# Three landing buffers instead of four for the streamed weights of a two-block transformer kernel

## The reference

```python
for layer in range(2):                       # first_block
    x = x + 0.5 * swiglu(rmsnorm(x), ffn1_w_in, ffn1_w_out)
    x = x + (attn_lru_mixer, deltanet_mixer)[layer](rmsnorm(x))
    x = x + cross_attention(rmsnorm(x), rmsnorm(mem))
    x = x + 0.5 * swiglu(rmsnorm(x), ffn2_w_in, ffn2_w_out)
x = rmsnorm(x)
for i in range(4):                           # second_block
    u = rmsnorm(x)
    x = x + rmsnorm((retention, conformer_conv, gla)[i % 3](u))
    x = x + rmsnorm(sq_relu_mlp(rmsnorm(x), mlp_w_up[i], mlp_w_down[i]))
```

## Time and profile before

| what | value |
|---|---|
| median of the 3 runs | 2798.34 us (2797.26 to 2812.16) |
| the profiled execution's own time | 2798.34 us |
| its span, first to last instruction | 2796.6 us |
| granted TensorE clock over the span, share of full speed | 0.991 |
| PEld busy | 2605.9 us (93%) |
| DVE busy | 1810.6 us (65%) |
| ACT busy | 1410.2 us (50%) |
| weight transfers | 836 of 512 KB |
| weight queue, share of the 16 DMA engines' span | 48.9% |

### The profile page before, as it was taken

The page is one execution under the profiler, slowest core; times in us unless marked ns, Lnnn a source line. Parts: engine busy times, 40 slices in busy tenths (PEclk is TensorE's granted clock), DMA queues, the critical chain, the costliest instruction groups (busy, mean ns, idle before and its releaser), DMA issues. The chain is left out here.

```text
span 2796.6 us, 49287 instructions
## 1 busy us (share of the span) xinstructions
PE 2700.4 (97%) x21142; PEld 2605.9 (93%) x21142; DVE 1810.6 (65%) x2351; ACT 1410.2 (50%) x1928; POOL 0.2 (0%) x4
## 2 busy tenths in 40 slices
PE   7999999999998889999999999989999999999998
PEld 7999899999988889999899999879988899989998
DVE  5657766666657646666646856968555675755764
ACT  5445555454466355545445565354454544446443
POOL 0000000000000000000000000000000000000000
PEclk9999999999999999999999999989999999999999
DMA  6554546655544234655544554226642465444463
GB/s 222 177 188 144 180 134 204 196 189 189 189 129 124 76 121 136 197 186 172 182 135 145 183 194 158 68 102 190 202 148 93 149 201 197 160 149 151 160 196 120
DMA packets 129002, 450.13 MB, mean 161 GB/s; under 512 B 20112, under 2 KB 20368, under 8 KB 128528
## 3 DMA queue, kind: packets, MB, share of 16 engines
q1 hardware_dynamic: 128784, 446.96, 48.9%
HBM read 445.47 MB, written 1.44 MB: 160 GB/s over the span
## 5 line engine op out<-in xcount | busy, mean ns | idle before, releaser
L262 PE MATMUL B<-R,WH 128*128 128x256 f32 x10432 | 2077.5, 282 | 33.7 <-DVE WL L965 24.7
L262 PEld LDWEIGHTS B<-R,WH 128*128 128x128 f32 x10432 | 1673.2, 189 | 50.7 <-issue 21.9
L965 DVE TENSOR_TENSOR WL<-SL,WH 128x1024 fp32r<-128x1024 f32 x836 | 1009.4, 1223 | 743.1 <-ACT WH L2007 742.4
L262 PE MATMUL B<-R,WL 128*128 128x256 f32 x4480 | 1253.7, 280 | 0.0
L2007 ACT ACTIVATE WH<-SL 128x1024 fp32r<-128x1024 f32 x836 | 865.2, 1052 | 526.8 <-PE B L262 506.8
L262 PEld LDWEIGHTS B<-R,WL 128*128 128x128 f32 x4480 | 846.2, 189 | 0.0
L262 PE MATMUL B<-RB,WH 128*128 128x256 f32 x1984 | 553.4, 279 | 0.8 <-DVE WL L965 0.8
L262 PE MATMUL B<-RB,WL 128*128 128x256 f32 x1728 | 481.1, 278 | 0.0
L262 PEld LDWEIGHTS B<-RB,WH 128*128 128x128 f32 x1984 | 371.9, 187 | 1.3 <-DVE WL L965 1.0
L262 PEld LDWEIGHTS B<-RB,WL 128*128 128x128 f32 x1728 | 324.3, 188 | 0.0
L262 PE MATMUL B<-WH,R 128*128 128x512 f32 x480 | 159.5, 403 | 0.9 <-DVE WL L965 0.9
(11 more groups left out here) (282 smaller groups left out, 1572.4 us busy)
## 6 DMA issues: line engine op xcount, KB each, us to landing
SL<-in_w SPq DMA_DIRECT2D x836, 512.0 KB, 3.6
CP<-in_cp SPq DMA_DIRECT2D x5, 768.0 KB, 5.0
X<-in_xT SPq DMA_DIRECT2D x2, 512.0 KB, 6.6
PG<-in_mem SPq DMA_DIRECT2D x1, 1024.0 KB, 10.8
out<-X SPq DMA_DIRECT2D x1, 1024.0 KB, 3.9
PK<-in_pk SPq DMA_DIRECT2D x1, 594.5 KB, 3.7
dn_y<-PG SPq DMA_DIRECT2D x1, 256.0 KB, 2.2
PG<-dn_y SPq DMA_DIRECT2D x16, 16.0 KB, 2.1
```

What stands on the lines that cost most here:

```text
L262: return p.matmul(o, left, right, start=first, stop=final, skip_group_check=True)
L965: v.tensor_tensor(WL[t % NSPL][:, :], SL[t % NRAW][:, :], WH[t % NSPL][:, :].bitcast(F32), ALU.subtract).then_inc(s_lo, 1)
```

## The change

The number of raw buffers is lowered from four to three. `NRAW` also is the number of landing semaphores `s_w`, and it stands in the indices and counts of lines 2004, 2007, 965 and 2800 to 2802. The number of split buffers, `NSPL`, stays at four. No instruction is added, removed or moved in any engine's list. What differs is the buffer that a tile lands in, and the condition of the wait in line 2801: tile t now waits for `lo(t - 3)` where it waited for `lo(t - 4)`. The transfer of tile 3, which was issued without a wait, now waits for `lo(0)`. The program uses 4 KB less in each of the 128 partitions.

```diff
@@ -118,7 +118,7 @@
     ST, NBLOCKS = stage_table()
     NTILES = w.shape[0]
     assert NBLOCKS == 4 * NTILES
-    NRAW, NSPL = 4, 4
+    NRAW, NSPL = 3, 4
```

## The result

In the comparison the changed kernel took 2820.9 us (median, 2807.9 to 2830.5), the kernel before 2802.8 us (2788.4 to 2812.2); the ratio is 1.0063, 95% interval [1.005, 1.0077]. That is above the range of 2799 to 2818 us. Two further measurements of the changed kernel, each beside the kernel before, gave 1.0035 [1.0018, 1.0053] and 1.006 [1.0048, 1.0072]. The mean of the three is 1.0053, or 14.8 us; the forecast was 9.0 us. The reference moved as well: 2798.34 us was the median of three runs, and the later medians of the kernel before were 2800.4 to 2807.9 us.

The account below looks back on a forecast made before the run. PE, busy for 97% of the span, was taken as the bound, so delays cost only where they reach it. Five terms summing to 9.0 us, on 2798.34 us, gave 2807.3 us; 2799 to 2818 us should hold 8 times in 10.

Parts of the forecast that it names:

- the steady stretches don't see it: Where PE sets the pace, three buffers still leave about 2.8 us to spare, so no change is seen.
- no transfer gets slower: Tile t's transfer starts when that of t + 1 started before, and takes what that one took.
- forecast marks: ACT's waits for landings grow from 19.7 us to 80 to 150 us, in some 70 to 100 waits instead of 15.
- The rival of the starving lockstep: Tile pairs in mN.up lose time to late transfers, 2827 us; 21% for it or a milder form, above 2812.
- Term 1: Starts of m0.up to m3.up: the late fourth high part delays PE 1.0 us in each, 4.0 us.
- My own rule: The `lo` that released the transfer of tile t + 1 before now releases that of tile t.
- Term 2: Start of c.in: same pattern as the starts of m0.up to m3.up, passing through DVE's convolution work to PE, 1.2 us.
- Term 3: m2.dn: a high part 1.6 us late reaches PE at its 0.80 us wait at 2331.89 us; 1.6 us.
- Term 4: xk0 and ab.g: a late high part holds up an evacuation, with a chain of gates behind it, by 0.6 us.
- Term 5: Later in m0.up to m3.up: one long lone transfer per stage is 1.6 us late, a quarter counted; 1.6 us in all.
- Other tiles come late by the same reckoning: Tiles in r0.v0, r3.v0, r0.o, r3.o and g.o come up to 3.7 us late, under 4 to 6 us of cover; no cost.

Follow-up runs that it names:

- k_before1: The kernel before with four raw buffers, unchanged, profiled again; the profiled execution took 2801.64 us.
- n_rest2: Kernel before, four buffers, but all tiles wait for `lo(t - 3)` except 80 to 84 and ten at the starts of m0.up to m3.up and c.in; ratio 1.0026.
- h_m2dn: Kernel before, four buffers, but only tiles 687 and 688 in m2.dn wait for `lo(t - 3)`; 2801.34 us.

## Why the prediction was wrong, step by step

The table is an account over all matmuls in order: for each, how much later than its predecessor it starts than in `k_before1`, sorted by whether PE stood idle, ran at half clock, or neither (pace). Each column is the mean of one kernel's profiles, in us. Where the line between an idle time and a slow step is drawn moves up to 1.5 us between the first row and the third.

| | before (5) | changed (3) | difference |
|---|---|---|---|
| PE idle | 0.9 | 10.8 | +9.9 |
| half clock | 1.5 | 5.7 | +4.2 |
| pace | -0.3 | 2.0 | +2.2 |
| profiled time | 2803.9 | 2820.2 | +16.3 |

*That the steady stretches don't see it, and that no transfer gets slower: right.* 86 waits and 138.4 us for landings were within the forecast marks, and they are the cover in use. (6.2 less 3.6 is 2.6 us to spare, not 2.8, which changes nothing. The stage m1.up had two more gaps in the trace before than the one of 0.17 us, 0.31 and 0.59 us at its start; none repeats.) The rival of the starving lockstep is out: after 1919 us PE waits for no low part in m1.up. The Trainium skill's mark of too few buffers (Perfetto Trace Analysis, "Identifying Performance Opportunities"), a gap that keeps repeating, is not seen on PE there.

*Term 1, the starts of m0.up to m3.up, 4.0 us: the mechanism right, the size low.* It is 5.6 us. I took only the fourth tile to be late; the third is too, and makes the fourth 2.4 to 2.6 us late instead of 2.1, in m1.up 3.1. My own rule gives the third: its transfer starts where that of the fourth started before, too late for a high part right behind the second. In m1.up a part comes from other tiles: with only the ten issued early (`n_rest2`), PE still has 0.9 us of added idle time there. In m1.up SP issues 768 KB for CP 4 us before these tiles; whether that is the reason for the 3.1 was not tried.

*Term 2, c.in, 1.2 us: the size low by half.* 2.3 us. I followed the lateness to the first wait of PE and stopped; it is taken up again twice.

*Term 3, m2.dn, 1.6 us: wrong.* It rested on a wait that a single trace had. In that trace PE ran at the short distance up to 2328 us and had caught up with ACT; in `h_m2dn` it ran at 117.8 ns and ACT waited for it.

*Term 4, xk0 and ab.g, 0.6 us: right.* PE waits for the gates in ab.g, 0.70, 0.21 and 0.43 us in the three profiles of the changed kernel and not at all in the five before:

```profile
299.75 1.63 PE L452 MATMUL B<-PK,BIG 128*128 128x128 f32 x12 [0.70 <-ACT PG L2239]
```

*Term 5, long transfers in mN.up, 1.6 us: not seen there*, but its size stands about right for other places, 0.3 to 0.6 us each near 319, 1393 and 2464 us; that long transfers cause these is not shown.

*What failed most: the list behind "Other tiles come late by the same reckoning", and that such tiles "meet 4 to 6 us of cover and cost nothing".* The end of ab.v is not in the list. By the same reckoning tiles 80 and 81 would have been 1.1 and 0.7 us late: in the trace before the transfers of 81 and 82 landed at 245.85 and 248.28, and the high parts of 80 and 81 started at 244.71 and 247.53. That is what the trace after shows. Their own cover holds: PE did not wait for their low parts. But in DVE's list there stands work behind them that PE wants sooner than the tiles, and I did not ask for its cover. It costs 0.4 to 0.8 us of idle time, and then in most executions a granted clock of 0.50, about 3 us together. The sum had no term for the clock at all, neither here nor behind 54 us, where two of the three profiles lose 1.5 us more. Of the 4.2 us of half clock in the table, 2.8 are lost at 264 us and 1.0 behind 54 us. The Trainium skill (TensorE: Matmul & The Clock Gate, "HAM oscillation — how this bites in real kernels") describes a kernel whose matmuls run at half rate after PE has waited for data, and counts the penalty of the slowed matmuls beside the wait itself. The traces agree that there are two costs: 0.77 us of wait, and 4.31 us for the 16 small matmuls behind it, 2.88 where the clock held. The waits in the page's example are far longer; here 0.57 to 0.83 us came ahead of the half clock. For a term of the sum I needed the place, and that only the timelines give.

*The reference.* 4.4 us of the 13.6 us between forecast and result are the difference between 2798.34 and the 2802.77 us of the comparison. As a share, the top of the stated range was 0.70% above the kernel before, and the 0.63% of the comparison lies under it. So the range was missed in part because its base was a quick execution; the cost itself was 18.1 us in the comparison and 14.8 in the mean of three, where 9.0 were forecast. The forecast had given 22% to more than 0.5%. It is luck that the 1.6 us too many of term 3 make up for part of the 2.7 that terms 1 and 2 lacked.

What stays open: whether three buffers also make the quicker pace rarer. Its three profiles have 84, 170 and 140 us in stretches at the short distance, 131 in the mean; the five of the kernel before have 186, with 0 to 412 in single ones. The 2.2 us of the table may be chance. What decides between the two distances, and how long the half clock lasts behind 54 us, is open too.

## What to carry to other kernels

When a buffer goes, walk the list of every engine that waits for it, and ask of each item behind the wait who wants it and when; the tile itself may have cover where its neighbour has none. Where two tiles in a row come late, the second one's lateness contains the first's. Before a wait of under a microsecond becomes a term, look for it in a second profile of the same kernel.

## What the runs showed of the hardware

PE's 256-column matmuls run at one of two distances, 113.3 or 117.8 ns from start to start, at the same granted clock of 1.00. With one exception in 18 traces the distance changed only where PE had stood idle or the row of matmuls had a step of 0.2 us or more. It goes with most of the spread of the five profiled executions of the kernel before: they took 2796 to 2813 us, and at the long distance throughout they would have taken 2808 to 2815 by an estimate with 4.0 us for each 100.

An idle time of 0.57 to 0.83 us ahead of small matmuls (64x128) was followed by a granted clock of 0.50 in seven of seven traces, one of 0.42 or 0.45 us in none of two. Nine traces don't show that the length of the idle time decides. Longer ones ahead of large matmuls, such as 1.11 us at 1582 us, were not followed by it.
